# A decoder layer's first projection tiles on x without its root, and their weights in two loads

## The reference, cut to what matters

```python
def _rmsnorm(x, g):
    y = x32 * lax.rsqrt(jnp.mean(x32 * x32, axis=-1, keepdims=True) + EPS)
    return (y * g).astype(x.dtype)

u = _rmsnorm(h, g_mix)                     # h: [280, 1024]
proj = u @ w_in                            # w_in: [1024, 2576]
xa, ya, q, k, v, g, lr = jnp.split(proj, split_idx, axis=-1)
xc = conv_b + sum(xa_ext[:, j:j + T] * conv_w[j] for j in range(CONV_W))
r_logit = einsum(xc, w_rg_a) + b_rg_a      # the gates of the RG-LRU
la = log_sigmoid(lr @ w_gate_up + b_gate) / GATE_TAU
```

## Time and profile before

| | |
|---|---|
| median of 3 runs | 1084.52 us (1084.24 to 1084.65) |
| the profiled execution | 1082.98 us, of which the span 1081.2 us |
| TensorE busy | 1051.6 us (97%) |
| VectorE, ScalarE busy | 325.2 us (30%), 193.7 us (18%) |
| HBM read | 422.82 MB, 393 GB/s over the span |

### The profile page before, as it was taken

The page is one execution under the profiler, slowest core; times in us unless marked ns, Lnnn a source line. Parts: engine busy times, 40 slices in busy tenths (PEclk is TensorE's granted clock), DMA queues, the critical chain, the costliest instruction groups (busy, mean ns, idle before and its releaser), DMA issues.

```text
span 1081.2 us, 13427 instructions
## 1 busy us (share of the span) xinstructions
PE 1051.6 (97%) x5387; PEld 435.7 (40%) x5387; DVE 325.2 (30%) x663; ACT 193.7 (18%) x317; POOL 15.0 (1%) x39
## 2 busy tenths in 40 slices
PE   7999999999999999999999799999999999999996
PEld 5758573333333333333333233333333333333332
DVE  6854342212222222222222222222222222122224
ACT  3453332111111111111111011111111111110112
POOL 4100000000000000000000000000000000000000
PEclk9999999999999999999999899999999999999998
DMA  9751689999999999999999999999999999999994
GB/s 313 267 183 47 258 361 390 424 428 420 430 429 432 433 430 427 435 434 430 429 432 433 427 432 430 432 432 433 426 436 431 432 431 433 430 432 432 433 419 162
DMA packets 34730, 425.59 MB, mean 394 GB/s; under 512 B 5351, under 2 KB 12350, under 8 KB 19594
## 3 DMA queue, kind: packets, MB, share of 16 engines
q1 hardware_dynamic: 33816, 424.50, 93.2%
q10 hardware_dynamic: 370, 0.39, 0.1%
q0 software_dynamic: 512, 0.26, 0.1%
HBM read 422.82 MB, written 2.35 MB: 393 GB/s over the span
## 4 chain that ended last, share of the span: by engine, by line
PE 70%; DMA 28%; issue 1%; DVE 1%; SPq 0%; ACT 0%; DVEq 0%
PE ps L1572 28%; DMA mem<-in_w_gu 27%; PE ps L1591 14%; PE ps L1290 6%; PE ps L1544 5%; PE ps L1614 4%; PE ps L1449 3%; PE ps L1638 2%; PE ps L1551 1%; PE ps L1336 1%; PE ps L1598 1%; DMA mem<-in_w_in 1%; PE ps L1631 1%; PE ps L1474 0%; PE ps L1329 0%
## 5 line engine op out<-in xcount | busy, mean ns | idle before, releaser
L1572 PE MATMUL ps<-mem 128*64 128x512 f32 x2048 | 461.2, 598 | 11.8 <-issue 6.3
L1572 PEld LDWEIGHTS ps<-mem 128*64 128x64 f32 x2048 | 142.2, 137 | 288.0 <-issue 275.2
L1591 PE MATMUL ps<-mem 128*64 128x512 f32 x1024 | 225.6, 593 | 0.6
L1171 DVE TENSOR_TENSOR mem<-ps,bguT 128x512 f32<-128x512 f32 x64 | 41.2, 686 | 373.0 <-PE ps L1638 373.0
L1591 PEld LDWEIGHTS ps<-mem 128*64 128x64 f32 x1024 | 74.7, 137 | 145.7 <-issue 145.7
L1201 DVE TENSOR_TENSOR yacc<-ps,yacc 128x1024 f32<-128x1024 f32 x64 | 75.5, 1219 | 131.3 <-PE ps L1614 131.3
L753 ACT ACTIVATE mem<-ps 128x512 f32<-128x512 f32 x32 | 19.1, 597 | 384.5 <-PE ps L1544 383.5
L1544 PE MATMUL ps<-mem 128*64 128x512 f32 x372 | 85.1, 592 | 0.0
L1290 PE MATMUL ps<-mem 128*128 128x280 f32 x256 | 64.0, 408 | 1.7 <-DMA mem<-in_w_in 1.7
L1614 PE MATMUL ps<-mem 64*128 64x512 f32 x256 | 64.1, 617 | 0.8 <-issue 0.8
L1153 DVE TENSOR_TENSOR mem<-slot_no,pos 128x192 f32<-128x192 f32 x32 | 11.5, 358 | 165.5 <-PE ps L1544 165.5
(11 more groups left out here) (320 smaller groups left out, 517.6 us busy)
## 6 DMA issues: line engine op xcount, KB each, us to landing
mem<-in_w_gu SPq DMA_DIRECT2D x58, 4096.0 KB, 24.8
mem<-in_w_down SPq DMA_DIRECT2D x18, 4096.0 KB, 26.7
mem<-in_w_down SPq DMA_DIRECT2D x26, 2048.0 KB, 24.1
mem<-in_w_gu SPq DMA_DIRECT2D x12, 2048.0 KB, 12.3
mem<-in_w_in SPq DMA_DIRECT2D x5, 2048.0 KB, 16.2
mem<-in_w_out SPq DMA_DIRECT2D x1, 4096.0 KB, 13.9
mem<-in_w_down SPq DMA_DIRECT2D x4, 1024.0 KB, 20.3
mem<-in_state_gla SPq DMA_DIRECT2D x8, 128.0 KB, 2.2
```

What stands on the lines that cost most here:

```text
L1171: dve.tensor_tensor(hS[:, n, :].rearrange("p (k s) -> p k s", k=8), turned[:, n], bguT[:, 8 * n:8 * n + 8, bass.ds(e_of(i - 1), 1)].broadc ...
L1572: last = pe.matmul(ps[S * w:S * w + S, n, :], xT[:, k % 4, k // 4, :], weights[:, col:col + 512], start=(k == 0), stop=(k == KD - 1))
L1591: last = pe.matmul(ps[S * w:S * w + S, bank, :], acts[:, k, :], weights[:, col:col + 512], start=(k == 0), stop=(k == KD - 1))
```

## The change

Root and gain are taken apart. The turned x, times its gain only, goes to a new buffer `xg`: ScalarE does it for x0 in eight pieces, VectorE for x1 and x2 in one instruction each. x0, x1 and x2 are turned in this order, into banks of their own. Tiles 0 and 1 are projected from `xg` (`project_raw`), and VectorE multiplies them by `rbc` as it takes them out of PSUM, in place of ScalarE's `take`. `uT`, which all other matmuls read, is now `xg` times `rbc`, in two instructions of four k each. The parameter transposes of the gains move to the front. `wxa` is loaded in two halves of four k, 1 MB each.

```diff
-        FRONT = {"x": 4, "roots": 5, "parameters": 6}
+        FRONT = {"first parameters": 1, "x0, four blocks": 2, "x0": 3, "x1": 4, "x2": 5, "roots": 6, "parameters": 7}
+        GAINED = {"x1": 1, "x2": 2, "uT": 4}
+        EARLY_TILES = range(2)
...
-            load(wxa, win[:, :, 0:512], "in_xa")
+            for n in range(2):
+                load(wxa[:, 4 * n:4 * n + 4], win[:, 4 * n:4 * n + 4, 0:512], ("in_xa", "in_xb")[n])
...
             square_x(0, sq_act)
+            act.wait_ge(sem("par_ready"), 1)
+            for k in range(KD):
+                act.wait_ge(sem("front_turned"), FRONT["x0, four blocks" if k < 4 else "x0"])
+                act.activation(xg[:, k, 0:P], ps[:, k // 4, (k % 4) * P:(k % 4 + 1) * P], ACT.Copy, scale=pv[:, G_MIX + k:G_MIX + k + 1]).then_inc(sem("xg_ready"), 1)
...
-            act.activation(rbc[:, 0:P], ps[:, 5, 280:280 + P], ACT.Copy).then_inc(sem("rbc_ready"), 1)
-            act.activation(rbc[:, P:NT], ps[:, 4, 280:280 + NT - P], ACT.Copy).then_inc(sem("rbc_ready"), 1)
+            act.activation(rbc, ps[:, 5, 0:NT], ACT.Copy).then_inc(sem("rbc_ready"), 1)
...
-            take(0, ACT.Copy)
             act.wait_ge(sem("z_abs"), 1)
...
-            take(1, ACT.Copy)
+            act.wait_ge(sem("proj_act"), len(EARLY_TILES))
             take(2, ACT.Copy)
...
+            gains = pv[:, G_MIX:G_MIX + KD].unsqueeze(2)
+            dve.wait_ge(sem("front_turned"), FRONT["x1"])
+            dve.tensor_tensor(xg[:, :, P:2 * P], ps[:, 2:4, :].rearrange("p a (k t) -> p (a k) t", t=P), gains.broadcast_to([P, KD, P]),
+                              ALU.mult).then_inc(sem("uT_ready"), 1)
+            dve.wait_ge(sem("front_turned"), FRONT["x2"])
+            dve.tensor_tensor(xg[:, :, 2 * P:NT], ps[:, 4, 0:KD * TL].rearrange("p (k t) -> p k t", k=KD), gains.broadcast_to([P, KD, TL]),
+                              ALU.mult).then_inc(sem("uT_ready"), 1)
             scale_x(0, 1)
             scale_x(2, 2)
             scale_x(1, 3)
...
-            dve.wait_ge(sem("rbc_ready"), 2)
-            for k in K_ORDER:
-                dve.scalar_tensor_tensor(out=uT[:, k, :], in0=ps[:, k, 0:NT], scalar=pv[:, G_MIX + k:G_MIX + k + 1], in1=rbc,
-                                         op0=ALU.mult, op1=ALU.mult).then_inc(sem("uT_ready"), 1)
+            dve.wait_ge(sem("rbc_ready"), 1)
+            dve.wait_ge(sem("xg_ready"), KD)
+            dve.wait_ge(sem("uT_ready"), GAINED["x2"])
+            for n in range(2):
+                half = slice(4 * n, 4 * n + 4)
+                dve.tensor_tensor(uT[:, half, :], xg[:, half, :], rbc.unsqueeze(1).broadcast_to([P, 4, NT]), ALU.mult).then_inc(sem("uT_ready"), 1)
+            for t in EARLY_TILES:
+                dve.wait_ge(sem("proj_done"), t + 1)
+                dve.tensor_tensor(proj[:, TILES[t][2], :], ps[:, bank_of(t), 0:NT], rbc, ALU.mult).then_inc(sem("proj_act"), 1)
...
+            pe.wait_ge(sem("in_xa"), 16)
+            pe.wait_ge(sem("xg_ready"), KD)
+            pe.wait_ge(sem("uT_ready"), GAINED["x2"])
+            project_raw(0, range(4))
             pe.wait_ge(sem("zeroed"), 2)
...
+            spread_root(0)
+            spread_root(1)
+            spread_root(2).then_inc(sem("front_turned"), 1)
+            project_raw(1, range(4))
+            pe.wait_ge(sem("in_xb"), 16)
+            project_raw(0, range(4, KD))
+            project_raw(1, range(4, KD))
...
-            project(0, K_ORDER[4:])
...
-            for t in XA_TILES[1:]:
+            for t in XA_TILES[2:]:
                 project(t)
```

More of the change, by code:

```diff
@@ L193, in hybrid_layer_kernel @@
         diag = first.cut(TC, P)
+        xg = flat(raw[:, 2:4, :])[:, 0:KD * NT].rearrange("p (k n) -> p k n", k=KD)
         third = Area(flat(raw[:, 2:4, :]))
@@ L867, in scale_x @@
                 dve.tensor_scalar(diag[:, c, :], ident[:, :], rstd[:, c:c + 1], None, ALU.mult).then_inc(sem("diag_ready"), 1)
+            dve.wait_ge(sem("front_turned"), FRONT["first parameters"])
+            dve.tensor_copy(pv[:, 0:CONV_W], ps[:, 7, 288:288 + CONV_W]).then_inc(sem("par_ready"), 1)
             dve.wait_ge(sem("x1_in"), 16)
@@ L871, in _ @@
                                      accum_out=ssq[:, 1:2]).then_inc(sem("sq1_x"), 1)
+            dve.wait_ge(sem("par_ready"), 1)
+            gains = pv[:, G_MIX:G_MIX + KD].unsqueeze(2)
[5 more added lines that the diff above has]
+                              ALU.mult).then_inc(sem("uT_ready"), 1)
             scale_x(0, 1)
@@ L874, in _ @@
             scale_x(1, 3)
-            dve.wait_ge(sem("front_turned"), FRONT["x"])
-            dve.tensor_copy(pv[:, 0:CONV_W], ps[:, 7, 288:288 + CONV_W]).then_inc(sem("par_ready"), 1)
-            dve.wait_ge(sem("par_ready"), 1)
             lam = pv[:, LAM:LAM + MA]
             dve.scalar_tensor_tensor(out=la0, in0=lam, scalar=-1.0, in1=lam, op0=ALU.mult, op1=ALU.max).then_inc(sem("lam_abs"), 1)
-            dve.wait_ge(sem("rbc_ready"), 2)
-            for k in K_ORDER:
-                dve.scalar_tensor_tensor(out=uT[:, k, :], in0=ps[:, k, 0:NT], scalar=pv[:, G_MIX + k:G_MIX + k + 1], in1=rbc,
-                                         op0=ALU.mult, op1=ALU.mult).then_inc(sem("uT_ready"), 1)
+            dve.wait_ge(sem("rbc_ready"), 1)
[7 more added lines that the diff above has]
+                dve.tensor_tensor(proj[:, TILES[t][2], :], ps[:, bank_of(t), 0:NT], rbc, ALU.mult).then_inc(sem("proj_act"), 1)
             dve.wait_ge(sem("lam_exp"), 1)
@@ L915, in _ @@
             link(dve.tensor_scalar(ta, la, 0.0, 1.0 / TAU, ALU.min, ALU.mult))
-            dve.wait_ge(sem("uT_ready"), KD)
+            dve.wait_ge(sem("uT_ready"), GAINED["uT"])
             dve.memset(uX[:, :, NM + NB:32], 0.0).then_inc(sem("uX_ready"), 1)
@@ L1263, in turn_x, with spread_root @@
                 for k in range(KD):
-                    last = pe.transpose(ps[:, k, c * P:c * P + r], yacc[0:r, c, k * P:(k + 1) * P], ident[0:r, 0:r])
+                    out = ps[:, 4, k * r:(k + 1) * r] if c == 2 else ps[:, 2 * c + k // 4, (k % 4) * P:(k % 4 + 1) * P]
+                    last = pe.transpose(out, yacc[0:r, c, k * P:(k + 1) * P], ident[0:r, 0:r])
+                    if c == 0 and k == 3:
+                        last.then_inc(sem("front_turned"), 1)
                 last.then_inc(sem("front_turned"), 1)
-            def spread_root(c, out):
-                return pe.matmul(out, ones[0:rows_of[c], :], diag[0:rows_of[c], c, 0:rows_of[c]], start=True, stop=True)
+            def spread_root(c):
+                r = rows_of[c]
+                return pe.matmul(ps[:, 5, c * P:c * P + r], ones[0:r, :], diag[0:r, c, 0:r], start=True, stop=True)
@@ L1271, in _, with project_raw @@
+            def project_raw(t, ks):
+                for k in ks:
+                    last = pe.matmul(ps[:, bank_of(t), 0:NT], TILES[t][1](k), xg[:, k, :], start=(k == 0), stop=(k == KD - 1))
+                if KD - 1 in ks:
+                    last.then_inc(sem("proj_done"), 1)
             pe.wait_ge(sem("ident_ready"), 1)
+            pe.wait_ge(sem("first_par_in"), 32)
+            pe.transpose(ps[:, 7, 288:288 + CONV_W], pin[0:CONV_W, :], ident[0:CONV_W, 0:CONV_W]).then_inc(sem("front_turned"), 1)
@@ L1272, in _ @@
             pe.wait_ge(sem("x0_in"), 32)
             turn_x(0)
-            pe.wait_ge(sem("first_par_in"), 32)
-            pe.transpose(ps[:, 7, 288:288 + CONV_W], pin[0:CONV_W, :], ident[0:CONV_W, 0:CONV_W]).then_inc(sem("front_turned"), 1)
+            pe.wait_ge(sem("x1_in"), 16)
+            turn_x(1)
             pe.wait_ge(sem("x2_in"), 32)
             turn_x(2)
-            pe.wait_ge(sem("x1_in"), 16)
-            turn_x(1)
+            pe.wait_ge(sem("in_xa"), 16)
+            pe.wait_ge(sem("xg_ready"), KD)
@@ L1280, in _ @@
+            pe.wait_ge(sem("uT_ready"), GAINED["x2"])
+            project_raw(0, range(4))
             pe.wait_ge(sem("zeroed"), 2)
-            pe.wait_ge(sem("diag_ready"), 2)
-            spread_root(0, ps[:, 5, 280:280 + P])
-            spread_root(2, ps[:, 4, 280 + P:280 + P + TL])
             pe.wait_ge(sem("diag_ready"), 3)
-            spread_root(1, ps[:, 4, 280:280 + P]).then_inc(sem("front_turned"), 1)
+            spread_root(0)
+            spread_root(1)
+            spread_root(2).then_inc(sem("front_turned"), 1)
@@ L1292, in project @@
                     last.then_inc(sem("proj_done"), 1)
[L1294 to L1297, removed]
             pe.wait_ge(sem("in_lr"), 16)
-            pe.wait_ge(sem("uT_ready"), KD)
+            pe.wait_ge(sem("uT_ready"), GAINED["uT"])
             for j in range(2):
```

## The result

| | before | after |
|---|---|---|
| median | 1084.34 us (16 runs, 1081.85 to 1087.53) | 1086.76 us (16 runs, 1084.83 to 1090.88) |
| the profiled execution | 1082.98 us, span 1081.2 us | 1087.21 us, span 1085.5 us |

The ratio of the runs is 1.0021, with a 95% interval from 1.0011 to 1.003: the change costs between 1.2 and 3.3 us, 2.4 by the medians, where 1.4 was forecast. By the bound of 0.2% this stands on the edge between no change and slower. Single runs lie up to 4 us from the median of their kernel; the 0.41 us between the first three runs of before, on which the prediction leaned, were a narrow sample. Two of the 17 runs of before that were taken beside e6_lr_early were slow ones of 1841 and 3460 us and are left out of every comparison.

What follows compares the result with a forecast made beforehand. TensorE's chain, fed by one 2 MB load, bounds the front. TensorE gains 2.5 us, but the gates await VectorE's convolution (+5.6 less 4.3, plus 0.1): +1.4, forecast 1085.9 us, counted as no change, range 1083.6 to 1088.2.

Steps and rivals of the forecast that it cites:

- TensorE's start: Tile 0's first matmul on TensorE: at 10.7 us, 3.0 earlier than before, when the first half of the weights lands.
- Slow passes: Tile 0's first eight matmul passes at TensorE's lower clock: 0.46 us each, 3.7 in all; later passes 0.236.
- roots: Three root matmuls on TensorE behind tile 0's first four matmuls: 0.7 us, against 1.91 with waits before.
- VectorE's list: VectorE's in-order work: two products and the evictions of tiles 0 and 1 precede the series, making VectorE 5.6 us late.
- series: VectorE's softplus series, queued behind both evictions though it needs neither tile: starts at 21.5 us instead of 15.91.
- The low-rank copy: VectorE's copy behind the series' start: done at 25.1 us, with TensorE waiting 2.5 for it.
- The convolution: VectorE's convolution, needed by the gates: ends at 50.0 us instead of 44.40, 5.6 later less 4.3 of slack.
- The gates: TensorE's gate matmuls: start at 50.1 us instead of 48.72, waiting 1.4 for VectorE, the shift carried to the end.
- convolution ends before TensorE has done its qk tiles: A stated condition, before the gates, under which the prediction would be wrong; it expected TensorE to wait for the convolution.
- the sum: Whole kernel: TensorE alone -2.5 us, VectorE's convolution +1.3 and hand-over 0.1; the later counts, so +1.4.
- The clock's count: TensorE's slow passes: their count hardly differs from run to run, since three runs lay within 0.41 us.
- The clock up sooner: Rival for tile 0: transposes raise TensorE's clock, eight passes take 1.9 us; -1.8, total 1084.1; chance 0.12.

Runs made afterwards that it cites:

- e6_lr_early: e1_gap with the low-rank matmuls also moved ahead of tile 1's second half; 1081.68 us, ratio 0.9981 to the kernel before.
- e4_roots: The changed kernel with the root matmuls behind one matmul of tile 0 instead of four; 1086.12 us, ratio 1.0017 to the kernel before.
- e1_gap: The changed kernel with VectorE's evictions of tiles 0 and 1 moved behind the series, to its wait for ScalarE's logarithm; 1084.04 us, ratio 0.999 to before.
- e2_fill: The changed kernel with TensorE projecting tile 2 before its wait for the low-rank copy; 1087.43 us, ratio 1.0023 to the kernel before.
- e3_one_load: The changed kernel with the first weight columns in one 2 MB load again; 1088.72 us, ratio 1.0039 to the kernel before.

## Why the prediction was right, and where it was off

- **TensorE's start.** Forecast 10.7, found 11.02 and 10.96: the first half of the weights landed last, 0.3 later. The gained x, which was to be ready at 10.4, was no reserve: in e4_roots TensorE waited for it (L886) until 11.16. Slow passes 3.96 and 3.63 for 3.7, roots 0.93 for 0.7. Tile 1 was out at 21.6 and 21.2 instead of 21.0.
- **VectorE's list.** Forecast: covered products, two waits of some 2 us together, series at 21.5. Found: 2.4 us of waits, series at 22.02 and 21.62, 6.1 and 5.7 behind the 15.91 of the earlier trace rows. e1_gap divides that: 3.3 us are the evictions in front of the series, which the order alone costs; 2.4 (18.31) are left by the products that come later.
- **The low-rank copy** ended at 25.07 for 25.1, the series' later start made good by instructions that had taken 0.28 us before and now take 0.17. TensorE waited 1.8 in all for 2.5 (1.50 for the copy and 0.31 for a parameter load), having come later itself.
- **The convolution** ended at 49.95 and 49.55 for 50.0. The late value rows, the parameters and the loads on POOL and SyncE stayed hidden, as argued: from the gates to the output projection the first profile of after took the same 66.02 as both of before.
- **The gates**: forecast +1.4, found +1.84 and +0.39. In the first profile the slow passes after the wait held them, which the text named and priced (1.8, of which 1.4 hidden, +0.4). There they cost 1.6 (2.23 for 1.21 and 23.41 for 22.80), of which 0.3 shows: the gates start at 50.40, and the convolution alone would have let them start at 50.10. So the condition "convolution ends before TensorE has done its qk tiles" came true in one of two profiles, by that mechanism, and does not overturn the sum: in the other, and in e2_fill, where TensorE had time to spare, the gates waited for VectorE.
- **The size.** The forecast's +1.4 lies inside the measured 1.2 to 3.3; the median, 2.4, is more, and the term that is too small is the clock's. The sum took each slow stretch as it stood in one profile and gave the waits that the change makes +0.4 at most. The mean granted clock of each run is on record: after's 16 runs have 0.985 to 0.993, 14 of them 0.991 or less; the 45 runs of before for which it is listed, taken beside the experiments, have 0.991 to 0.995, 44 of them 0.992 or more. The three edits that keep the evictions in front of the series (e2_fill, e3_one_load, e4_roots), taken beside 30 of these, have medians of 0.990 to 0.992. The medians of after and before, 0.991 and 0.994, differ by 0.003 of 1085 us: by estimate 3.3 us of TensorE's time at full clock, a part of it under waits. After's three slowest runs (1089.37 to 1090.88) have its three lowest clocks (0.985 to 0.987). So the change does make slow passes likelier, and with the evictions moved (e1_gap) the median clock is back at 0.993 to 0.994. The profiles agree: between the forget gate and the first expert neither of before shows a lower clock, and six of the seven of after and its edits do (+1.34 and +1.76 in the table). Which of the waits, or what else in the new order, lowers it stays open: e6_lr_early, where TensorE does not wait on the way to the gates, shows 0.73 from 150 to 156 us.
- **The clock's count.** The prediction held that the count of slow passes hardly differs from run to run, from three runs' times. It differs: eight passes took 3.70 and 4.10 before, 3.96 and 3.63 after, 2.12 in e6_lr_early. The Trainium skill, TensorE: Matmul & The Clock Gate, Part 1, says so, and these rows agree with it. That these passes ran at the lower level is read from their length, about twice 0.236: the granted clock reads 1.00 over them in both profiles of both kernels. Only in e1_gap, where the eight took 3.28, does it show the lower level too (after's first profile has 1.00 in this window):

```profile
10.00:14.00 4.00, 3.19 (x9) 2.41 (x10) 1.40 (x8) 0.12 (x1) 3.38 (x7) 0.71 1.09 314
```

- **The clock up sooner.** Against this rival the prediction held the rule on transposes that it cites, and 0.46 a pass behind transposes. e6_lr_early's profile is against that rule: TensorE had done nothing but transposes, then waited 1.02, and its first eight passes took 2.12, where the rival said 1.9. So the rival can come true, and in the other profiles it did not; what decides stays open.

## What to carry to other kernels

Work that moves to an engine with an in-order list delays all that stands behind it there, by the arrival of its inputs more than by its own duration: two evictions of 0.45 us made the series 3.3 us later (21.62 beside e1_gap's 18.31). Put such work where the engine waits for something else anyhow (L938 in e1_gap), and put what another engine waits for (the low-rank matmuls) ahead of it. When a stage is held by another engine's chain, filling the first engine's waits only moves them (e2_fill).

## What the runs showed that was not expected

- The granted clock can fall or hold in the same place of the same kernel: behind the wait for the low-rank copy it read 0.50 in one profile of after (1.50 us in the bracket) and 1.00 in the other (1.18), and in two edits of it, behind waits of nearly the same length, four passes took 2.23 (e3_one_load, 1.88) and 1.21 (e4_roots, 1.87). It also fell to 0.63 in a stretch in which TensorE showed no wait at all (88 to 92 us).
- Two profiles of one unchanged kernel (before) differ by 2.2 us in their spans, of which 0.75 in the front.
- VectorE's 128x4 instructions of the series took 0.28 us each ahead of the low-rank copy before (L896) and 0.17 after (L914). Why was not tried.
